# The routing of a two-block transformer kernel: router product, ranks, row copies and the first expert load rearranged

## The chip, the cores and the metric

The kernel runs on one NeuronCore of one Trainium2 chip. A core has five engines that run beside each other and meet at semaphores: TensorE (PE: matrix products and transposes, into PSUM), VectorE (DVE), ScalarE (ACT), GpSimd (POOL) and SyncE (SP, which here only issues DMAs). ACT and POOL issue DMAs too. On-chip data lie in SBUF (128 partitions); PSUM has eight banks of 128 x 512 floats. The metric is the time of one execution on the device in microseconds (us).

## The reference, cut to what matters

Two blocks of two layers each run over 512 tokens of width 1024. The first block is an attention and Fourier mixer and a long convolution, each with a dense feed-forward part. The second block's two layers end in a mixture of experts with two-level routing, which the kernel computes twice (i = 0, 1):

```python
pg = softmax(hf @ router_g)                       # (512, 4), top-1 group
gi = argmax(pg)
le = (hf @ router_e).reshape(t, 4, 8)             # 32 experts in 4 groups of 8
pk, ik = top_k(softmax(le[gi]), 2)                # two experts in the chosen group
wts = pg[gi] * pk / sum(pk);  eid = gi * 8 + ik
order = argsort(flat_e)                           # 1024 (token, expert) pairs, sorted by expert,
dest = start_pad[se] + arange(n) - start_raw[se]  # packed into blocks of 128 rows of one expert
yb = map(lambda xi, e: (silu(xi @ w1[e]) * (xi @ w3[e])) @ w2[e], blocks)
y = segment_sum(yb * buf_w, buf_tok)
```

## The kernel before, in words

Every engine has its own program, written as a list of stages. Between two stages that are not `joined`, the four computing engines meet: each drains, adds one to `stage_end` and waits until all have done so. SP runs ahead and loads weights into a ring of four slots of 2 MB.

At the end of each mixer stands `Project` (output matrix, 512 x 1024 results added to x), then `Norm` (an RMS norm with modulation, from x to h), then `Route`, `Experts` and `Combine`. Before the change `Project` and `Norm` are joined, and a meeting stands between `Norm` and `Route`.

Activations lie transposed, as eight tiles of 128 channels by 512 tokens. `Norm.scalar` ends with one ACT operation for each tile of h (L535), which adds one to `tiles`.

`Route`, on the engines:

- ACT issues two DMAs for the router weights (1024 x 4 and 1024 x 32; L2489, L2490), does the two exponentials (L2492, L2494), stores h by rows in DRAM as `h_rows` (L2496), and at the end reads the table of pairs back (L2499).
- PE makes the logits with a 128 x 128 piece of h stationary and the 36 router columns moving: 4 token tiles x 8 k = 32 products of 36 columns (L2529). Then it turns h into rows (32 transposes in 8 groups of 4, L2537). After the choice of experts it makes the rank of each token within its expert: 10 products for "how many tokens before me" and 4 for the totals (L2542, L2545).
- DVE copies the logits from PSUM (L2587), takes the group maximum, and then copies the 8 groups of rows from PSUM (L2594) before it goes on with the choice: a chain of small operations, each followed by a drain (helpers at L2561 to L2572). After `hot_done` it waits for the ranks (L2635), works out where each pair goes (`dest_done`), and then, once `h_rows` is stored, the plan: which expert each of up to 40 blocks has, and how many steps there are (L2663).
- POOL writes number tables and zeros, fills the table in DRAM (L2515), and after `dest_done` scatters the 8 x 128 pairs into it (8 indirect DMAs, L2520).

`Experts` then handles two blocks a step: POOL gathers 128 token rows (L2780), PE turns them (L2850), ACT and DVE split activations and weights into a rounded high part and a low rest (L2924, L2934 on ACT; L554, L3006 on DVE), and PE does three products for each (L560). SP's loads of w1, w3 and w2 (2 MB each, L2746) start once all engines have met; the second waits until the first gather has landed. In the first routing POOL sends two scatters with nothing to write ahead of its first gather, which set the counts of the semaphores right.

`L` numbers in the rows are those of the kernel before.

## Time and profile before

| | us |
|---|---|
| median of 3 runs | 4682.4 (4681.4 to 4684.97) |
| the profiled execution, its own time | 4681.74 |
| its span in the profile | 4679.9 |
| PE busy | 3998.8 (85%) |
| DVE busy | 2899.0 (62%) |
| ACT busy | 1916.4 (41%) |
| POOL busy | 880.0 (19%) |

The span is what the profiler saw from the first to the last instruction; 1.8 us lie around it. The granted clock of TensorE is printed as a share of 2.4 GHz, so 0.50 is 1.2 GHz. An idle time in square brackets stands before the instruction of the row, with what ended it. A queue name with q (ACTq, SPq) is the engine's sequencer issuing a DMA: the duration is that of the issue. A matrix product or transpose in full fp32 precision may appear as two MATMUL records.

### The profile page before, as it was taken

To read this page: it belongs to the slowest core of one execution; us is meant where nothing else is said; L and a number is where in the kernel's file an instruction comes from. 1 tells how busy PE (TensorE), PEld (TensorE's weight loads), DVE (VectorE), ACT (ScalarE), POOL (GpSimd) and SP (SyncE) were. 2 spreads that over 40 slices of the span, in tenths; PEclk is the share of its full clock that TensorE was granted. 3 is DMA by queue.
4 is the path that set the end of the run, shared out by engine and by line. 5 is a ranking of instruction groups with operands and counts; after the bars stand their busy time and mean duration, and the time that the engine had idled before them with its cause. 6 is when DMAs were issued, how large, how long until landed. Compare 5 with 4: busy or idle time off the path is not lost. (4 is left out here: it accounts for less than half of the span.)

```text
span 4679.9 us, 52688 instructions
## 1 busy us (share of the span) xinstructions
PE 3998.8 (85%) x19060; PEld 3186.2 (68%) x19060; DVE 2899.0 (62%) x3435; ACT 1916.4 (41%) x2295; POOL 880.0 (19%) x460
## 2 busy tenths in 40 slices
PE   4988899778988999678888888769999695899995
PEld 3755677536645777578888888548888474788884
DVE  6754775337745874344444445459999443899995
ACT  2142432203103332343333333247777221777773
POOL 0200000002100000032222221025554001355551
PEclk9989999969999999789999999879999796999997
DMA  5421354303501452100000001079998311999993
GB/s 184 144 91 36 113 177 143 110 13 127 215 18 63 164 170 86 31 19 18 18 18 18 18 18 36 8 271 376 355 365 331 126 54 33 373 376 360 366 357 111
DMA packets 372150, 691.39 MB, mean 148 GB/s; under 512 B 38327, under 2 KB 118327, under 8 KB 371320
## 3 DMA queue, kind: packets, MB, share of 16 engines
q1 hardware_dynamic: 327696, 639.79, 38.5%
q10 hardware_dynamic: 25032, 32.98, 2.1%
q0 software_dynamic: 19296, 16.94, 1.1%
q8 instruction: 80, 1.31, 0.1%
q14 instruction: 46, 0.38, 0.0%
HBM read 700.01 MB, written 41.00 MB: 158 GB/s over the span
## 5 line engine op out<-in xcount | busy, mean ns | idle before, releaser
L560 PE MATMUL psum<-work_rounded 128*128 128x512 f32 x3504 | 1164.1, 402 | 94.7 <-DVE work_rounded L554 29.0
L554 DVE TENSOR_TENSOR ring_rounded<-ring,work_rounded 128x2048 fp32r<-128x2048 f32 (+1 forms) x445 | 816.0, 1836 | 408.8 <-ACT work_rounded L549 279.7
L560 PEld LDWEIGHTS psum<-work_rounded 128*128 128x128 f32 x3504 | 669.2, 192 | 266.2 <-issue 114.9
L560 PE MATMUL psum<-work_rounded,fixed_rounded 128*128 128x512 f32 x2544 | 782.5, 402 | 28.0 <-DVE fixed_rounded L3006 15.8
L560 PE MATMUL psum<-work_rounded,ring_rounded 128*128 128x512 f32 (+1 forms) x1824 | 726.0, 398 | 0.0
L549 ACT ACTIVATE work_rounded<-ring 128x1024 fp32r<-128x1024 f32 x204 | 214.5, 1057 | 1026.3 <-PE psum L560 697.9
L2924 ACT ACTIVATE work_rounded<-ring 128x2048 fp32r<-128x2048 f32 x256 | 490.9, 1919 | 274.9 <-PE psum L560 171.2
L560 PEld LDWEIGHTS psum<-work_rounded,fixed_rounded 128*128 128x128 f32 x2544 | 483.1, 190 | 146.4 <-issue 15.9
L560 PE MATMUL psum<-fixed_rounded,work_rounded 128*128 128x512 f32 (+1 forms) x1088 | 432.1, 397 | 0.0
L560 PEld LDWEIGHTS psum<-work_rounded,ring_rounded 128*128 128x128 f32 x1824 | 350.8, 192 | 78.5
L554 DVE TENSOR_TENSOR work_rounded<-work,work_rounded 128x2048 fp32r<-128x2048 f32 (+1 forms) x196 | 337.6, 1733 | 41.9 <-ACT work_rounded L2924 37.5
L370 DVE SCALAR_TENSOR_TENSOR work<-ring,fixed,work 128x512 f32<-128x512 f32 x392 | 318.7, 825 | 25.9 <-issue 0.9
L560 PE MATMUL psum<-ring_rounded,fixed_rounded 128*128 128x512 f32 x768 | 307.2, 400 | 0.0
L2924 ACT ACTIVATE work_rounded<-work 128x2048 fp32r<-128x2048 f32 x128 | 245.2, 1919 | 101.2 <-PE psum L560 82.9
L2786 POOL DMA_INDIRECT pair_rows<-work x66 | 174.0, 2637 | 562.0 <-DVE work L3016 560.0
L554 POOL TENSOR_TENSOR ring_rounded<-ring,ring_rounded 128x1024 fp32r<-128x1024 f32 x32 | 89.7, 2807 | 906.1 <-ACT ring_rounded L549 906.1
L560 PE MATMUL psum<-ring_rounded 128*128 128x512 f32 (+1 forms) x768 | 239.7, 373 | 9.2 <-DVE fixed_rounded L554 9.2
L560 PEld LDWEIGHTS psum<-fixed_rounded,work_rounded 128*128 128x128 f32 x1088 | 209.4, 192 | 47.4 <-issue 2.6
L554 POOL TENSOR_TENSOR ring_rounded<-ring,fixed_rounded 128x1024 fp32r<-128x1024 f32 x23 | 48.2, 2099 | 976.1 <-ACT fixed_rounded L549 976.1
L2780 POOL DMA_INDIRECT fixed<-h_rows,work x64 | 170.7, 2667 | 54.7 <-POOL work L2777 53.8
L2163 PE MATMUL psum<-work 128*128 128x128 f32 x1152 | 156.9, 279 | 26.8 <-ACT work L2266 26.8
L560 PEld LDWEIGHTS psum<-ring_rounded,fixed_rounded 128*128 128x128 f32 x768 | 146.4, 191 | 32.6
(317 smaller groups left out, 6029.9 us busy)
## 6 DMA issues: line engine op xcount, KB each, us to landing
ring<-in_w SPq DMA_DIRECT2D x128, 2048.0 KB, 13.8
work<-in_w SPq DMA_DIRECT2D x64, 2048.0 KB, 13.5
ring<-in_mod_w SPq DMA_DIRECT2D x24, 2048.0 KB, 8.6
ring<-in_ada_w SPq DMA_DIRECT2D x24, 2048.0 KB, 8.0
ring<-in_ffn_w_in SPq DMA_DIRECT2D x44, 1024.0 KB, 7.6
ring<-in_ffn_w_out SPq DMA_DIRECT2D x10, 2048.0 KB, 7.9
ring<-in_w_in_a SPq DMA_DIRECT2D x32, 512.0 KB, 6.0
ring<-in_hy_w_in SPq DMA_DIRECT2D x6, 2048.0 KB, 8.2
```

What stands on the lines that cost most here:

```text
L370: ins = dve.scalar_tensor_tensor(out=acc, in0=w[:, k, :], scalar=c.par(cond, k), in1=acc, op0=ALU.mult, op1=ALU.add)
L549: return act.activation(c.rounded(out), v, ACT.Copy)
L554: return eng.tensor_tensor(c.rounded(v), v, c.rounded(v_high), ALU.subtract)
L560: ins = pe.matmul(out, c.rounded(w), c.rounded(x), start=(start and i == 0), stop=(stop and i == 2))
L2163: ins = pe.matmul(c.pair(4 * l + 2, KEYS)[:, cols], A[:, t, :], TT[:, t, :], start=False, stop=True, skip_group_check=True)
L2780: pool.indirect_dma_start(self.g[:, b, :], None, self.c.d["h_rows"], bass.IndirectOffsetOnAxis(ap=self.gi[:, b:b + 1].bitcast(U32), axis=0 ...
L2786: pool.indirect_dma_start(self.c.d["pair_rows"], bass.IndirectOffsetOnAxis(ap=self.si[:, b:b + 1].bitcast(U32), axis=0), self.y_sb[:, b, : ...
L2924: act.activation(c.rounded(self.unit_high(o, u)), self.unit_raw(o, u), ACT.Copy).then_inc(self.made, 1)
```

## The change: the routing's products, copies and first load

- **Router product.** The 36 router columns become the stationary side and the 512 tokens of a tile of h stream past them: 8 products of 512 columns, each of which waits only for its own tile of h. The result has 36 partitions; DVE copies it to SBUF (`lg_rows`), and PE turns it in 4 transposes back to 128 tokens by 36, which DVE copies again. The router weights are fetched by ACT at the start of `Project.scalar`, into the buffer of the gathered rows (`M_G`), and `Norm` is joined to `Route`.
- **Rows.** The 8 copies of h's rows from PSUM move from DVE to ACT, four before the second exponential and four behind it.
- **Ranks.** DVE sums the one-hot choices over token tiles (4 small additions, `sums`), and two products of 160 and 128 columns replace the 14.
- **First load.** A new semaphore `planned` follows the plan; SP waits for that alone before it asks for the first w1 matrix, and for the meeting only after it. The plan's scratch no longer lies in the rows' buffer, so DVE doesn't wait for the store.
- **POOL.** It waits for the 8 router products before it clears `M_G`. In the first `Experts` the two empty scatters go behind the first two gathers.

```diff
@@ Project.scalar
+        if self.route:
+            self.route.fetch(act)
         c.arrived(act, self.n[0])
         self.parts.open_high(act, self.unit(0), self.unit(1))
@@ Route
-        self.rw = v(R_W, KD, 36)
+        self.rw = v(M_G, KD, 36)
+        self.lg_rows = v(M_HI, T)
+    def keep_rows(self, act, i):
+        act.wait_ge(self.turned, self.base["turned"] + i + 1)
+        act.activation(self.ht[:, i // 2, 512 * (i % 2):512 * (i % 2) + 512], self.c.ps[:, i % 4, :], ACT.Copy)\
+            .then_inc(self.turned_out, 1)
@@ Route.scalar
-        act.dma_start(self.rw[:, :, 0:GROUPS], ...).then_inc(self.w, 16)
-        act.dma_start(self.rw[:, :, GROUPS:36], ...).then_inc(self.w, 16)
         act.wait_ge(self.gsub, self.base["gsub"] + 1)
         act.activation(self.eg, self.eg, ACT.Exp).then_inc(self.gexp, 1)
+        for i in range(4):
+            self.keep_rows(act, i)
         act.wait_ge(self.esub, self.base["esub"] + 1)
         act.activation(self.e8, self.e8, ACT.Exp).then_inc(self.eexp, 1)
+        for i in range(4, 8):
+            self.keep_rows(act, i)
@@ Route.gpsimd
+        pool.wait_ge(self.logits, self.base["logits"] + 1)
@@ Route.tensor
-        for t in range(NT):
-            for k in range(KD):
-                ins = pe.matmul(c.ps[:, 6, 36 * t:36 * t + 36], c.h[:, k, P * t:P * t + P], self.rw[:, k, :],
-                                start=(k == 0), stop=(k == KD - 1))
+        for k in range(KD):
+            pe.wait_ge(self.norm.tiles, self.norm.tiles0 + k + 1)
+            ins = pe.matmul(c.ps[0:36, 6, :], self.rw[:, k, :], c.h[:, k, :], start=(k == 0), stop=(k == KD - 1))
+        ins.then_inc(self.logits, 1)
+        pe.wait_ge(self.rowed, self.base["rowed"] + 1)
+        for t in range(NT):
+            ins = pe.transpose(c.ps[:, 7, 36 * t:36 * t + 36], self.lg_rows[0:36, P * t:P * t + P],
+                               c.const("ident")[0:36, 0:36])
         ins.then_inc(self.logits, 1)
...
-        for t in range(NT):
-            for b in range(t + 1):
-                pe.matmul(c.ps[:, 7, 32 * t:32 * t + 32], c.const("before" if b == t else "ones"), self.both[:, b, :],
-                          start=(b == 0), stop=(b == t))
-        for t in range(NT):
-            ins = pe.matmul(c.ps[:, 7, 128:160], c.const("ones"), self.both[:, t, :], start=(t == 0), stop=(t == NT - 1))
+        pe.matmul(c.ps[:, 5, 0:32 * (NT + 1)], c.const("ones"), self.sums.rearrange("p t e -> p (t e)"),
+                  start=True, stop=False, skip_group_check=True)
+        ins = pe.matmul(c.ps[:, 5, 0:32 * NT], c.const("before"), self.both.rearrange("p t e -> p (t e)"),
+                        start=False, stop=True, skip_group_check=True)
@@ Route.vector
-        dve.tensor_copy(self.lg, c.ps[:, 6, 0:36 * NT].rearrange("p (t n) -> p t n", t=NT))
+        dve.tensor_copy(self.lg_rows[0:36, :], c.ps[0:36, 6, :]).then_inc(self.rowed, 1)
+        dve.memset(self.sums[:, 0, :], 0.0)
+        dve.wait_ge(self.logits, self.base["logits"] + 2)
+        dve.tensor_copy(self.lg, c.ps[:, 7, 0:36 * NT].rearrange("p (t n) -> p t n", t=NT))
...
-        for i in range(8):
-            dve.wait_ge(self.turned, self.base["turned"] + i + 1)
-            dve.tensor_copy(self.ht[:, i // 2, 512 * (i % 2):512 * (i % 2) + 512], c.ps[:, i % 4, :]).then_inc(self.turned_out, 1)
...
+        for t in range(NT):
+            tt(self.sums[:, t + 1, :], self.sums[:, t, :], self.both[:, t, :], ALU.add)
         dve.drain().then_inc(self.hot_done, 1)
...
-        dve.wait_ge(self.stored, self.base["stored"] + 16)
...
+        dve.drain().then_inc(self.planned, 1)
@@ Experts.sync
-        sp.wait_ge(self.c.stage_end, 4 * self.number)
+        sp.wait_ge(self.route.planned, self.route.base["planned"] + 1)
         first, more = self.steps(sp)
         load(0, first, 0, 0, True)
+        sp.wait_ge(self.c.stage_end, 4 * self.number)
         load(0, first, 0, 1, True, self.gather[0])
@@ Experts.gpsimd
-        if self.i == 0:
-            for b in range(2):
-                self.scatter_rows(pool, b)
...
         for b in range(2):
             self.gather_block(pool, 0, first, b)
+        if self.i == 0:
+            for b in range(2):
+                self.scatter_rows(pool, b)
@@ stages
-        project.norm = add(Norm(..., after=project))
-        add(Route(c, i))
+        project.norm = add(Norm(..., after=project), joined=True)
+        route = project.route = Route(c, i, project.norm)
+        add(route)
```

The order of TensorE's instructions at the first routing, from the last product of the norm (L471 in both) to the first transposes of `Experts`, in the kernel before:

```order
L471 MATMUL psum<-work,fixed 128x512 x5
L2529 MATMUL psum<-work,fixed 128x36 x32
L2537 MATMUL psum<-fixed 128x128 x32
L2542 MATMUL psum<-work,fixed 128x32 x10
L2545 MATMUL psum<-work,fixed 128x32 x4
L2703 TENSOR_LOAD work
L2703 ISA x2
L2850 MATMUL psum<-fixed 128x128 x8
```

The same place in the changed kernel:

```order
L471 MATMUL psum<-work,fixed 128x512 x5
L2548 MATMUL psum<-fixed 36x512 x8
L2552 MATMUL psum<-fixed,work 128x36 x4
L2560 MATMUL psum<-fixed 128x128 x32
L2563 MATMUL psum<-work,fixed 128x160
L2565 MATMUL psum<-work,fixed 128x128
L2726 TENSOR_LOAD work
L2726 ISA x2
L2873 MATMUL psum<-fixed 128x128 x8
```

32 router products of 36 columns became 8 of 512 and 4 transposes, and 14 rank products became two. ACT at the same routing, in the kernel before, from the last tiles of the norm (L535) on:

```order
L527 ACTIVATE work<-psum,fixed 128x512
L535 ACTIVATE fixed<-fixed 128x512 x8
L2489 DMA work<-in_router_g_2 128x8x4
L2490 DMA work<-in_router_e_2 128x8x32
L2492 ACT_TABLE_LOAD
L2492 ACTIVATE work<-work 128x16
L2494 ACTIVATE work<-work 128x32
L2496 DMA h_rows<-work 128x4x1024
L2499 DMA work<-table 128x42x2
```

In the changed kernel, there:

```order
L527 ACTIVATE work<-psum,fixed 128x512
L535 ACTIVATE fixed<-fixed 128x512 x8
L2505 ACT_TABLE_LOAD
L2505 ACTIVATE work<-work 128x16
L2499 ACTIVATE work<-psum 128x512 x4
L2509 ACTIVATE work<-work 128x32
L2499 ACTIVATE work<-psum 128x512 x4
L2513 DMA h_rows<-work 128x4x1024
L2516 DMA work<-table 128x42x2
```

The two DMAs of the router weights are gone from here (they stand ahead of the first L549 of `Project`), and the eight copies of 512 columns came in around the second exponential.

## Rows read from the trace of the kernel before

**Rows 1.** Stretches: us, busy PE, PEld, DVE, ACT, POOL; clock; DMA share; GB/s
```profile
3124.00:3142.00 18.00, 18.00 (x86) 14.76 (x85) 16.59 (x12) 13.94 (x11) 4.95 (x3) 1.00 1.04 396
3011.30:3028.77 17.47, 13.95 (x66) 13.98 (x67) 0.00 (x1) 1.30 (x2) 4.72 (x8) 0.50 0.09 12
```
**Rows 2.** Timeline of ACT, first routing: start, duration, instruction [idle before, releaser]
```profile
3005.57 5.75 ACT L535 ACTIVATE fixed<-fixed 128x512 f32<-128x512 f32 x8 [4.23 <-DVE fixed L503]
3011.43 0.40 ACTq L2489 DMA_DIRECT2D work<-in_router_g  x1
3011.86 0.60 ACTq L2490 DMA_DIRECT2D work<-in_router_e  x1
```
**Rows 3.** Timeline of PE, first routing
```profile
3014.82 13.84 PE L2529 MATMUL psum<-work,fixed 128*128 128x36 f32 x64 [14.21 <-DMA work<-in_router_e]
...
3046.22 4.48 PE L2542 MATMUL psum<-work,fixed 128*128 128x32 f32 x20 [12.15 <-DVEq L2631]
3050.51 1.90 PE L2545 MATMUL psum<-work,fixed 128*128 128x32 f32 x8
```
**Rows 4.** Timeline of DVE, first routing
```profile
3028.77 0.31 DVE L2587 COPY work<-psum 128x144 f32<-128x144 f32 x1 [19.01 <-PE psum L2529]
3029.15 0.17 DVE L2572 TENSOR_REDUCE work<-work 128x4 f32<-128x16 f32 x1
3029.40 0.17 DVE L2591 TENSOR_TENSOR work<-work 128x16 f32<-128x16 f32 x1
3029.60 0.69 DVE L2594 COPY work<-psum 128x512 f32<-128x512 f32 x1
...
3035.20 0.40 DVE L2572 TENSOR_REDUCE work<-work 128x4 f32<-128x16 f32 x2
...
3052.44 0.19 DVE L2635 COPY work<-psum 128x32 f32<-128x32 f32 x1 [6.35 <-PE psum L2545]
...
3061.87 0.18 DVE L2663 CAST work<-work 128x41 int32<-128x41 f32 x1
```
**Rows 5.** Lines L464 and L471, 512 columns: ns min/median/max, first and last start
```profile
L464 PE MATMUL psum<-fixed x5: 1011/1061/1061, 62.0 to 65.4; 128*128 128x512 f32 x5
...
L471 PE MATMUL psum<-work,fixed x10: 592/592/692, 2996.1 to 3000.0; 128*128 128x512 f32 x10
```
**Rows 6.** Stretches after PE starts on the first expert block, each routing
```profile
3092.65:3097.40 4.75, 4.75 (x12) 3.75 (x13) 0.50 (x1) 1.78 (x1) 0.19 (x1) 0.51 1.04 385
3989.40:3995.10 5.70, 5.70 (x14) 4.50 (x15) 1.83 (x2) 3.30 (x2) 0.00 (x0) 0.51 1.05 392
```
**Rows 7.** Timeline of POOL, end of each routing and start of the experts
```profile
3058.45 1.62 POOL L2520 DMA_INDIRECT table<-work  x1 [41.64 <-DVEq L2651]
...
3075.47 0.10 POOL L2803 MEMSET work<- 128x2 int32 x1 [6.56 <-ACTq L3200]
3077.30 1.00 POOL L2786 DMA_INDIRECT pair_rows<-work  x1 [1.72 <-issue]
...
3080.69 1.07 POOL L2780 DMA_INDIRECT fixed<-h_rows,work  x1 [0.90 <-POOL work L2777]
...
3108.61 2.79 POOL L2780 DMA_INDIRECT fixed<-h_rows,work  x1 [0.85 <-POOL work L2777]
...
3972.60 1.07 POOL L2780 DMA_INDIRECT fixed<-h_rows,work  x1 [0.89 <-POOL work L2777]
```
**Rows 8.** Timelines of PE and ACT, the first expert block of each routing
```profile
3086.78 1.97 PE L2850 MATMUL psum<-fixed 128*128 128x128 f32 x8 [34.38 <-DMA fixed<-h_rows,work]
3085.51 3.71 ACT L2924 ACTIVATE work_rounded<-ring 128x2048 fp32r<-128x2048 f32 x2 [45.86 <-DMA ring<-in_w]
...
3095.62 1.91 ACT L2924 ACTIVATE work_rounded<-ring 128x2048 fp32r<-128x2048 f32 x1 [5.42 <-DMA ring<-in_w]
...
3979.93 1.97 PE L2850 MATMUL psum<-fixed 128*128 128x128 f32 x8 [32.50 <-DMA fixed<-h_rows,work]
...
3991.80 1.91 ACT L2924 ACTIVATE work_rounded<-ring 128x2048 fp32r<-128x2048 f32 x1 [4.89 <-DMA ring<-in_w]
```

More of the change, by code:

```diff
@@ L649, in __init__ @@
         self.gate, self.keep = gate, keep
-        self.norm, self.leads = None, True
+        self.norm, self.leads, self.route = None, True, None
         self.tiles, self.tiles0 = core.shared("x_tile", KD)
@@ L2427 @@
 R_W = R_HT + NT * D
[L2428 to L2429 removed]
+R_SM = R_W
+R_END = R_SM + 4000
 M_KEEP = W0 + WORK - 256
@@ L2447, with __init__ @@
 class Route(Stage):
-    def __init__(self, core, i):
+    def __init__(self, core, i, norm):
         super().__init__(core)
-        self.i = i
-        self.per = {"w": 32, "turned": 8, "turned_out": 8, "stored": 16, "logits": 1, "gsub": 1, "gexp": 1,
+        self.i, self.norm = i, norm
+        self.per = {"w": 32, "turned": 8, "turned_out": 8, "stored": 16, "logits": 2, "rowed": 1, "gsub": 1, "gexp": 1,
                     "esub": 1, "eexp": 1, "rank": 1, "filled": 16, "placed": 128, "back": 16,
-                    "hot_done": 1, "dest_done": 1, "vals_done": 1}
+                    "hot_done": 1, "dest_done": 1, "vals_done": 1, "planned": 1}
         self.base = {}
@@ L2479, in __init__ @@
         self.both = new(NT, EXPERTS)
+        self.sums = new(NT + 1, EXPERTS)
         self.destf = new(2, NT)
@@ L2651, in vector @@
         dve.drain().then_inc(self.dest_done, 1)
-        planf, cmp = new(48), c.view(R_HT, BLOCKS, EXPERTS)
-        dve.wait_ge(self.stored, self.base["stored"] + 16)
+        planf, cmp = new(48), c.view(M_HI + T, BLOCKS, EXPERTS)
         tt(cmp, row(ends, BLOCKS, EXPERTS), col(iota[:, 0:BLOCKS], EXPERTS), ALU.is_le)
@@ L2674, with __init__ @@
     ROOM = 12
-    def __init__(self, core, i, weights):
+    def __init__(self, core, i, weights, route):
         super().__init__(core)
-        self.i = i
+        self.i, self.route = i, route
         self.w1, self.w3, self.w2 = (core.d[w][i] for w in weights)
```

21 lines of the change are left out of this document (11 added, 10 removed).

## The prediction, made before the changed kernel was run

> **What bounds the kernel now.** I read the stretches first. In the steady expert loop TensorE is busy 18.00 of 18.00 us at full clock [rows 1], so it is the bound there, and whatever the loop's start gains is kept to the end. During the router product the same view shows PE busy 13.95 of 17.47 us at clock 0.50, DVE idle and DMA at 0.09 [rows 1]: no overlap, one engine at a time. So I went on to the timelines of the routing, where everything is a chain: ACT finishes the tiles of h (3005.57 + 5.75 = 3011.32), issues the router DMAs, PE multiplies, DVE chooses, PE ranks, DVE places, POOL scatters, all meet, and the experts start with a matrix that is not there yet. ACT idles 45.86 us until the first w1 lands at 3085.51 and PE 34.38 us until the first gather lands at 3086.78 [rows 8]. The whole of this is on the path, so a microsecond cut from it is a microsecond of the result, twice, since there are two routings.
>
> **Logits.** Before: PE starts at 3014.82, after the router weights have come, and DVE has the logits at 3028.77 [rows 3, 4]. After: the weights are there, and the first product can start when tile 0 is done. ACT's eight tiles take 5.75 us, 0.72 each and the last one a little longer [rows 2], so tile 0 is there at about 3006.4. A product of 512 columns in fp32 is two records. At the slow clock records start (65.4 - 62.0)/4 = 0.85 us apart, at the fast clock (3000.0 - 2996.1)/9 = 0.43 [rows 5]: 1.7 or 0.86 us a product. Which clock? PE has been idle since the norm's last product (started 3000.0, 0.6 long), and in the stretch before the logits the clock is 0.50, 1.2 GHz [rows 1]. When the first expert block starts after such a pause, the clock stays at 0.51 for 4.75 us in one routing and 5.70 in the other [rows 6], and then is at 2.4 GHz. In between them and a somewhat earlier rise (this stream has no gaps) I take 4.3 us. Then 5 records go at 0.85, the other 10 steps at 0.43, and the last lasts 0.6: 4.3 + 4.3 + 0.6 = 9.2 us, until 3015.6. Behind it come DVE's copy from PSUM (0.69, as L2594 [rows 4]), four small transposes, some 0.7, and four crossings of 0.11 (PE ends at 3028.66, DVE starts at 3028.77 [rows 3, 4]) less the overlaps: DVE copies the logits at 3017.2. Gain 28.77 - 17.2 = **11.6 us**. Ends: never a fast clock, 15 x 0.85 + 1.06 = 13.9 us, gain 6.5; always fast, 15 x 0.43 + 0.6 = 7.1, gain 13.8. The end "always fast" needs the clock not to fall in the 5.7 us pause.
>
> The Trainium skill (TensorE: Matmul & The Clock Gate, "What's actually happening") says that the slow state is the default and that activity releases it, at a moment that varies with where the stream begins. Rows 6 agree: 4.75 and 5.70 us for the same code.
>
> **Rows copied by ACT.** DVE's copies lie between 3029.57 (end of L2591) and 3035.20 [rows 4], 5.63 us. What was hidden under them now shows: the wait for the first exponential, two crossings and an operation of 0.17, together 0.4. Gain **5.2 us**. On ACT four copies must be over when DVE asks for the second exponential, about 17 small operations of 0.25 us (3029.15 to 3029.40 [rows 4]) or 4.2 us after the first. Four copies at ACT's pace of 0.72 [rows 2] take 2.9 and PE turns the rows beside them, so they fit. The other four run beside some 7 us of DVE's chain. If they didn't fit, the cost is one or two copies, 1.4 us. The store of h_rows goes out earlier than before in any case.
>
> **Ranks.** From 3046.22 to 3052.44, 6.2 us [rows 3, 4]. 28 records in 6.2 us are 0.22 each. The new ones are four: two of 160 columns and two of 128; by the slow clock of rows 5 (0.85 for 512) 0.27 and 0.21, in all 1.0, plus 0.2 to drain. Gain **5.0**. Against it stand four additions on DVE with their drains, 4 x 0.25 = **1.0**. The memset of 32 columns lies beside the transposes.
>
> So the point where POOL starts its scatters (3058.45 [rows 7]) comes 11.6 + 5.2 + 5.0 - 1.0 = 20.8 us earlier, in both routings: 41.6. POOL's own clearing now starts with the products' end instead of 3011.4, but has 18 us until POOL is needed.
>
> **The first w1.** The plan is done at 3062.05 [rows 4], and stays at that distance behind the placing. SP waited for the meeting at about 3075.4 [rows 7] and the matrix landed at 3085.51, 10.1 us later [rows 8]. With the same 10.1 it now lands at 3072.2 on the old scale, before the meeting. ACT can split it at once; the experts then hang on the first gather and on w3, which SP asks for only when that has landed. Two costs and two gains:
> - POOL's scatters into the table run beside the 2 MB load. Below: nothing. Above: the last one can't be held beyond the landing of the matrix plus its own time, 3072.2 + 2 against the 3070 or so of before, 3.5 us. The packets are tiny and few, so I take 0.5, twice 0.5 = **-1.0**.
> - In the first routing the gather is issued at 3080.69 behind two empty scatters that begin at 3077.30; two of them are 2.3 us [rows 7]. It then lands 6.1 us after issue (3086.78), beside the matrix. Alone it should be faster: at least 1.07 to issue plus a quarter of the matrix's 8.5 us (a quarter of the bytes), 3.2; at most 6.1. I take 4.5: landing at 3078.4 + 4.5 = 3082.9, gain **3.8**. w3 follows it as before (8.8 us, 3086.78 to 3095.62 [rows 8]).
> - In the second routing there are no scatters: issue 3972.60, landing 3979.93. With 4.5 it is 2.8 earlier. w3 took 11.9 us there (3979.93 to 3991.80), which I put down to w1 still being under way; with the 8.8 of the first routing 3.1 less. Gain **5.9**.
> - PE's part: block 0 needs w1's products before w3's; with the gather at 3082.9 they have time. I count no more gain than w3's arrival gives: **+9.7** for both. Below: 0 if the gather isn't faster and w3 slower; above: 3.2 instead of 4.5 twice, +12.3.
>
> The Trainium skill (DMA: Bandwidth & Descriptors, "Queues, rings and completion order") says that a DMA engine goes round between its queues packet by packet. By that rule a scatter waits for a packet of the load and not for the load: the first cost would be near nothing, and the sum 1 us better. No row of this trace shows a scatter beside a load.
>
> A row speaks against the start: POOL's gather takes 1.07 us while DVE is idle, but 2.79 at 3108.61 while DVE splits weights [rows 7]. Now ACT splits w1 right after the meeting, and DVE follows some 2 us later, when the first gather is already issued and only the second and the scatters remain. If DVE were earlier, 1.7 us a routing are lost. The Trainium skill (GPSIMD Engine Reference, "8. Key points") names it: POOL shares its SBUF interfaces with DVE where DVE has two SBUF inputs.
>
> **The fetch.** The two DMA issues now stand ahead of ACT's first operation of `Project`, which starts right after a meeting or a mixer, with DVE and PE waiting for it: 3011.43 to 3012.46 is 1.03 us [rows 2], twice: **-2.1**. Below zero cost isn't possible; above, small-packet traffic beside nothing else costs nobody.
>
> **The sum.** 41.6 - 1.0 + 9.7 - 2.1 = 48.2 us. From the profiled execution's 4681.7 (span 4679.9 and 1.8 around it) that is 4633.5; the median is 0.7 above this execution, so 4634.
>
> **Rivals.**
> - *The slow clock holds.* TensorE stays at 1.2 GHz through both products, each 5.1 us longer: 4634 + 10 = 4644. For it: with 36 columns the clock stayed at 0.50 for 17 us [rows 1]. Against: those were short products, and the 512-column streams of rows 6 brought the clock up within 5.7 us.
> - *The early matrix gives nothing.* The gather takes its 6.1 us as before, w3 its time, and the scatters are held the full 3.5 us: 4634 + 9.7 - 2.3 + 6 = 4647. For it: w3, not w1, is what ACT waits for second, and the code still holds it back until the gather lands. Against: the gather had the matrix beside it before.
> - *Slower: the loop gets out of step.* The loads, released by PE and ACT, run at DMA share 1.04 beside a TensorE that is full [rows 1]. If the new order at the start leaves the loads one slot later for good, each of the 64 expert blocks waits for a matrix. From 48.2/64 = 0.75 us a block on, the change is slower; at 1 us a block the time is 4634 + 64 = 4698. Against: after the start ACT never waits for a load in the loop, and the slots are freed in an unchanged order.
>
> **Chances.** The forecast 0.78 (own range 4626 to 4641), the slow clock 0.09, no gain from the matrix 0.10, slower 0.03. The range for 8 in 10: low 4625 (fast clock 2.2 twice, the shorter gather 2.6, and some us more if the ranks start at the fast clock), high 4649, which takes in both faster rivals. What can be told from no change is 0.2%, 9.4 us: both mild rivals are clearly faster, so faster 0.95, same 0.02, slower 0.03.
>
> **What would show it.** In the changed profile: the 8 router products start before the last tile of the norm is done and end some 9 us later, with a clock change among them; DVE's copy of the 128 x 144 logits about 11 us sooner behind the norm; no 128 x 512 copies on DVE in the routing; two rank products in about 1.2 us; the first w1 issued before the meeting, so that ACT's first split of weights waits for the meeting alone; the next wait of ACT, for w3, about 9 us behind the gather. It is wrong if PE's products take nearly 14 us, if the last scatters or the table's reading take longer than the 17 us from first scatter to meeting, if `Project` starts much later than 1 us after its meeting, or if an expert period is no longer 18.0 us.

## Result: 41 us of the 48 forecast, ratio 0.991

The changed kernel takes 4642.72 us (median; 4642.01 to 4643.43) against 4683.68 (4681.4 to 4688.73) of the kernel before on the same chip: ratio 0.9911, 95% interval 0.9894 to 0.9928. A second comparison gave 4643.6 against 4683.89, ratio 0.9916 (0.9899 to 0.9933). The forecast was 4634, range 4625 to 4649. The gain is 41.0 us (40.3 the second time) where 48.2 were forecast. The time lies inside the stated range, but outside the 4626 to 4641 that the prediction gave to its own mechanism.

The profile after has a span of 4641.6 us, 38.3 less than before. Its rows answer to the groups of before in turn. First the stretches (columns as in [rows 1]): the first 4.06 us and the last 4.30 of the router products, and one period of the steady loop.

```profile
3012.64:3016.70 4.06, 4.06 (x5) 0.89 (x6) 3.22 (x6) 4.06 (x7) 0.00 (x0) 0.50 0.02 4
...
3017.70:3022.00 4.30, 4.26 (x10) 0.90 (x8) 0.00 (x0) 1.03 (x1) 0.00 (x0) 1.00 0.00 0
3124.00:3142.00 18.00, 18.00 (x86) 14.76 (x85) 16.59 (x12) 13.95 (x12) 9.34 (x5) 1.00 1.04 395
```

The loop is what it was (ACT starts on a block 17.98 us after the one before in both traces). During the router products PE no longer stands alone: ACT's tiles (4.06 us) and DVE's norm (3.22) lie beside them, and between the two stretches the clock has gone from 1.2 to 2.4 GHz, where it stayed at 0.50 before [rows 1]. ACT's timeline, first routing, with the same columns as [rows 2]:

```profile
3011.68 5.75 ACT L535 ACTIVATE fixed<-fixed 128x512 f32<-128x512 f32 x8 [4.23 <-DVE fixed L503]
...
3024.18 2.04 ACT L2499 ACTIVATE work<-psum 128x512 f32<-128x512 f32 x4
3029.42 0.23 ACT L2509 ACTIVATE work<-work 128x32 f32<-128x32 f32 x1 [3.19 <-DVE work L2632]
...
3060.54 0.37 ACTq L2516 DMA_DIRECT2D work<-table  x1
3066.95 3.71 ACT L2947 ACTIVATE work_rounded<-ring 128x2048 fp32r<-128x2048 f32 x2 [35.36 <-PEq L2864]
...
3081.62 3.71 ACT L2947 ACTIVATE work_rounded<-ring 128x2048 fp32r<-128x2048 f32 x2 [7.16 <-DMA ring<-in_w]
```

3011.68 is the zero of all distances below; before it was 3005.57 [rows 2]. The first split of w1 now waits for the meeting and no longer for a DMA [rows 8]; the second, of w3, still waits 7.16 us for one. PE's timeline, answering to [rows 3] and [rows 8]:

```profile
3012.64 9.32 PE L2548 MATMUL psum<-fixed 128*36 128x512 f32 x16 [5.92 <-ACT fixed L535]
3022.74 0.44 PE L2552 MATMUL psum<-fixed,work 36*128 36x36 f32 x4 [0.78 <-DVE work L2608]
...
3037.28 0.90 PE L2563 MATMUL psum<-work,fixed 128*128 128x160 f32 x2 [10.35 <-DVEq L2654]
3037.98 0.64 PE L2565 MATMUL psum<-work,fixed 128*128 128x128 f32 x2
...
3071.86 1.54 PE L2873 MATMUL psum<-fixed 128*128 128x128 f32 x6 [33.25 <-DMA fixed<-h_rows,work]
```

Sixteen records in 9.32 us, and both rank products over in 1.3. (The last row is cut where its window ends: the block's eight transposes take 1.97 us, as before.) DVE's, answering to [rows 4]:

```profile
3023.22 0.31 DVE L2611 COPY work<-psum 128x144 f32<-128x144 f32 x1 [0.49 <-PE psum L2552]
...
3025.05 1.09 DVE L2589 TENSOR_SCALAR work<-work 128x16 f32<-128x16 f32 x1
...
3038.65 0.19 DVE L2658 COPY work<-psum 128x32 f32<-128x32 f32 x1 [1.50 <-PE psum L2565]
```

The logits are copied 11.54 us behind the zero (before 23.20), the ranks 26.97 (before 46.87). POOL's, answering to [rows 7]:

```profile
3024.30 1.81 POOL L2531 MEMSET work<- 128x2048 f32 x1
...
3044.66 1.62 POOL L2539 DMA_INDIRECT table<-work  x1 [17.12 <-DVEq L2674]
...
3054.17 0.96 POOL L2539 DMA_INDIRECT table<-work  x1 [0.30 <-issue]
3065.48 0.10 POOL L2827 MEMSET work<- 128x2 int32 x1 [10.35 <-ACTq L3224]
...
3067.70 1.08 POOL L2804 DMA_INDIRECT fixed<-h_rows,work  x1 [0.94 <-POOL work L2801]
```

A table of the distances, in us from the start of the norm's tiles on ACT, each read from a timeline's start. "Step 2's first block" is ACT's start on the activations of the third expert block (L2934 before, L2957 after); from there on the steady loop runs.

| | before | after | moved |
|---|---|---|---|
| logits copied, 1st / 2nd routing | 23.20 / 23.05 | 11.54 / 10.76 | 11.66 / 12.29 |
| first scatter issued | 52.88 / 52.21 | 32.98 / 31.24 | 19.90 / 20.97 |
| table read back | 64.99 / 63.94 | 48.86 / 46.80 | 16.13 / 17.14 |
| first gather issued | 75.12 / 71.11 | 56.02 / 53.97 | 19.10 / 17.14 |
| PE turns the first block | 81.21 / 78.44 | 60.18 / 57.33 | 21.03 / 21.11 |
| ACT splits the first w3 | 90.05 / 90.31 | 69.94 / 67.42 | 20.11 / 22.89 |
| step 2's first block | 120.39 / 121.76 | 101.43 / 99.81 | 18.96 / 21.95 |

From first scatter to the table's reading the kernel gives 3.8 us back in each routing (12.11 and 11.73 before, 15.88 and 15.56 after). A second profile of the changed kernel has 15.36 and 15.43 there, so 3.3 to 3.8; its step 2 begins at 101.43 and 99.84, within 0.03 us of the first profile's. That is the largest difference from the forecast, and the experiments began there.

### The profile page after: what moved, and what is told of

Read it like the earlier page. It is cut to its first block and busy times, and to the rows that moved or that the text cites. A ratio compares the mean times of both kernels' runs of the same rounds, so it can differ in the third digit from the quotient of the medians.

```text
span 4641.6 us, 52428 instructions
## 1 busy us (share of the span) xinstructions
PE 3979.8 (86%) x18924; PEld 3153.0 (68%) x18924; DVE 2889.9 (62%) x3431; ACT 1924.3 (41%) x2311; POOL 885.9 (19%) x460
## 3 DMA queue, kind: packets, MB, share of 16 engines
q10 hardware_dynamic: 25032, 32.98, 2.1%
## 5 line engine op out<-in xcount | busy, mean ns | idle before, releaser
L549 ACT ACTIVATE work_rounded<-ring 128x1024 fp32r<-128x1024 f32 x204 | 214.6, 1057 | 1029.3 <-PE psum L560 698.0
L2947 ACT ACTIVATE work_rounded<-ring 128x2048 fp32r<-128x2048 f32 x256 | 490.9, 1919 | 260.4 <-PE psum L560 175.3
L2947 ACT ACTIVATE work_rounded<-work 128x2048 fp32r<-128x2048 f32 x128 | 245.2, 1919 | 101.3 <-PE psum L560 83.0
```

The lines of the kernel that those rows point to most:

```text
L549: return act.activation(c.rounded(out), v, ACT.Copy)
L2947: act.activation(c.rounded(self.unit_high(o, u)), self.unit_raw(o, u), ACT.Copy).then_inc(self.made, 1)
```

## Experiments

"Gain" is against the kernel before on the same chip. The intervals of the ratios are some 8 us to either side, so small differences between kernels are read from the distances in their traces. `e1` to `e4` were compared with one set of runs of the kernel before, median 4687.68, and gain some 2 to 4 us more than the changed kernel's 41.0 and the distances of their step 2 give; their gains are not compared with those of the changed kernel.

| run | median us | gain | ratio, 95% |
|---|---|---|---|
| `e1_w1_late` | 4647.31 | 40.4 | 0.9915 (0.9898 to 0.9932) |
| `e2_w1_after_scatters` | 4639.37 | 48.3 | 0.9899 (0.9883 to 0.9916) |
| `e3_w3_free` | 4638.66 | 49.0 | 0.9896 (0.9880 to 0.9913) |
| `e4_warm_clock` | 4641.90 | 45.8 | 0.9907 (0.9890 to 0.9923) |
| `e5_w1_scat_w3_free` | 4632.75 | 51.1 | 0.9891 (0.9874 to 0.9907) |
| `e6_warm_blocks` | 4633.78 | 50.1 | 0.9893 (0.9876 to 0.9909) |
| `e7_dve_rows` (one run) | 4649.9 | 34.0 | |
| `e8_clear_moved` (one run) | 4641.51 | 43.2 | |
| `e9_best` | 4629.23 | 55.5 | 0.9878 (0.9862 to 0.9895) |
| `e10_old_products` (one run) | 4661.17 | 23.6 | |
| `e11_best_no_norm_warm` | 4630.05 | 54.7 | 0.9883 (0.9867 to 0.9900) |

### The first w1 behind the meeting again

```diff
     def sync(self, sp):
-        sp.wait_ge(self.route.planned, self.route.base["planned"] + 1)
+        sp.wait_ge(self.c.stage_end, 4 * self.number)
         first, more = self.steps(sp)
         ...
         load(0, first, 0, 0, True)
-        sp.wait_ge(self.c.stage_end, 4 * self.number)
```

> The changed kernel with the first w1 asked for after the meeting again. Theory A (the early 2 MB load holds back the completion of the table's scatters): from the first scatter to the reading of the table 12.1 us as in the kernel before, not 15.9 as in the changed one, so the meeting comes 3.8 us sooner; against it the first gather again runs beside w1 (6 to 7 us from issue to TensorE's first transpose, not 3.4 to 4.2), and w3 follows it. Net in the first routing about 2.7 us sooner at the first block, in the second about 1.9 us later, so the total is within 2 us of the changed kernel's 4642.7. Rival B (the later reading of the table has another cause, such as the order on GpSimd or the earlier store of the rows): the 15.9 us stay, and all of the start's gain is lost, some 8 us slower than the changed kernel, 4650.

From first scatter to the table's reading it takes 12.04 and 11.75 us, as before the change: the 3.8 us are the load's. At the start of the experts it loses what the scatters win: step 2's first block begins at 102.60 and 100.99, 1.2 us later than in the changed kernel in both routings, and from the gather's issue to PE's turn is 8.15 and 7.03 us in place of 4.16 and 3.36. PE turns the first block within 0.3 us of when it does in the changed kernel; it is ACT that then waits for w1, whose split starts 1.5 and 2.9 us behind that turn. A first routing 2.7 us sooner, as expected, is not there. So the early matrix, as the change has it, is worth 1.2 us a routing and not the 4 to 5 forecast.

### The first w1 behind the last scatter

```diff
         sp.wait_ge(self.route.planned, self.route.base["planned"] + 1)
+        sp.wait_ge(self.route.placed, self.route.base["placed"] + 16 * 8)
```

> The changed kernel with the first w1 asked for when the plan is there and the eight scatters have landed. Theory A: 12.1 us from the first scatter to the reading of the table; w1 asked for at about the same moment, landing some 4 us behind the meeting, while the gather has it beside it only for its last 2 us. First block about 3 us sooner in each routing than in the changed kernel: 4636 to 4638. Rival B (another cause of the late reading): 15.9 stay and w1 comes later for nothing, 4644 or more. Rival C: the load now holds back the reading of the table instead (from 4.9 us to 7 or more), and the total stays at 4642.

The view of DMA issues, for the changed kernel in the stretch with the first routing's scatters (count, KB each, median us from issue to landing):

```profile
table<-work POOLq DMA_INDIRECT x8
work<-table ACTq DMA_DIRECT2D x1, 42.0 KB, 4.9
```

and for this one:

```profile
table<-work POOLq DMA_INDIRECT x8, 2.6
work<-table ACTq DMA_DIRECT2D x1, 42.0 KB, 6.0
```

The median landing of 2.6 us is that of scatters with no load beside them; for the changed kernel the view gives no figure. In this kernel the eight take 12.05 and 11.74 us again. The load now meets the next small transfer instead: the table's reading takes 6.0 us in place of 4.9 in the first routing (POOL is at the gather 8.27 us after it, before 7.16); in the second, where the load starts a little later behind it, nothing is lost (7.34 against 7.17). Step 2's first block begins 0.47 and 3.61 us sooner than in the changed kernel, where 3 were expected in each routing. PE's turn is 2.29 and 2.84 us sooner; in the first routing 1.82 of that is lost behind it, with 19.4 us at 1.2 GHz up to step 2 in place of 13.7.

The changed kernel's DMA while the load lies on the scatters (columns of [rows 1]; the last two are DMA share and GB/s):

```profile
3049.80:3052.00 2.20, 0.00 (x0) 0.00 (x0) 0.00 (x0) 0.00 (x0) 1.59 (x3) 0.50 0.81 15
...
3054.00:3058.00 4.00, 0.00 (x0) 0.00 (x0) 0.00 (x0) 0.00 (x0) 0.96 (x1) 0.50 1.05 374
3058.00:3060.50 2.50, 0.00 (x0) 0.00 (x0) 0.00 (x0) 0.00 (x0) 0.00 (x0) 0.50 0.39 117
```

POOL's issues keep their pace (0.96 us each, the last at 3054.17), so POOL isn't held; the packets are. The trace's records of single DMA packets show it. Each scatter has 32. Those of the first four come 1.5 to 2.2 us behind their issue, the last of them at 3050.86. The load's packets begin at 3050.88. The fifth scatter is issued at 3050.38, but none of its packets comes before 3056.16, 4.2 us late; the 128 packets of the last four scatters then lie among the load's. The last of them is at 3059.86, the last of the load at 3059.85. In the second routing the same gap goes from 3924.50 to 3930.08, and the ends are 3933.22 and 3933.64; there the load, issued at 3923.82, has its first packet only at 3926.93, later than the fifth scatter was due by its issue. With the load behind the scatters all eight come 1.27 us apart without a gap. So the scatters end with the load. This is the bound that the prediction worked out (3.5 us: "beyond the landing of the matrix") and set aside.

### The first w3 without its wait for the gather

```diff
-        load(0, first, 0, 1, True, self.gather[0])
+        load(0, first, 0, 1, True)
```

> The changed kernel with w3 asked for right after the meeting, not after the first gather. Theory A: w3 is what the first block waits for: ScalarE starts to split it 10 to 11 us after the meeting and not 16; the gather beside it takes 6 us and not 4. Products of w1 begin 2 us later, those of w3 follow without a pause: 2 to 3 us sooner in each routing, 4637 to 4639. Rival B (the gather, not w3, decides): the slower gather costs 2 us in each routing, 4646 or more.

ACT's timeline of the first routing, L2947 being the splits of w1 and of w3:

```profile
3066.20 3.71 ACT L2947 ACTIVATE work_rounded<-ring 128x2048 fp32r<-128x2048 f32 x2 [34.96 <-PEq L2864]
...
3077.22 3.70 ACT L2947 ACTIVATE work_rounded<-ring 128x2048 fp32r<-128x2048 f32 x2
```

w3's split waits for no DMA any more, and the gather pays: 7.81 and 7.08 us from issue to PE's turn in place of 4.16 and 3.36. In all, step 2's first block begins 2.25 and 2.29 us sooner. From PE's turn to that block are 35.78 and 36.29 us, against 41.25 and 42.48 in the changed kernel. The clock differs too: in the first routing of the changed kernel it falls twice more after the first slow stretch, in this kernel once; in all it is at 1.2 GHz for 10.5 and 11.2 us in place of 13.7 and 18.4.

The changed kernel from PE's first turn on:

```profile
3071.80:3079.00 7.20, 6.53 (x19) 5.22 (x20) 2.98 (x3) 1.20 (x2) 4.45 (x5) 0.52 0.83 267
3079.00:3085.30 6.30, 3.21 (x14) 2.25 (x12) 1.73 (x1) 3.68 (x2) 0.00 (x0) 1.00 1.04 381
3085.30:3088.80 3.50, 2.80 (x7) 2.25 (x8) 2.76 (x2) 1.91 (x3) 0.00 (x0) 0.53 1.05 386
3088.80:3099.30 10.50, 6.96 (x35) 5.44 (x34) 6.88 (x6) 7.94 (x6) 3.52 (x3) 0.99 1.04 399
3099.30:3102.30 3.00, 3.00 (x8) 2.30 (x7) 3.00 (x2) 0.94 (x2) 0.00 (x0) 0.50 1.05 388
```

PE is busy 3.21 of 6.30 us while it waits for w3, and behind that the clock is at 1.2 GHz again for 3.5 us; after a stretch with 6.96 of 10.50 it is there again for 3. Here the gap cost its own length, and slow products stand behind it.

What the slow stretches cost can be read from the kernels that have the same expert code and load order as the changed one. From PE's first turn to step 2 they take, by routing:

| kernel | us | of these at 1.2 GHz |
|---|---|---|
| `e8_clear_moved` | 40.11 / 42.60 | 11.3 / 18.7 |
| changed | 41.25 / 42.48 | 13.7 / 18.4 |
| changed, second profile | 41.52 / 42.63 | 14.1 / 18.5 |
| `e7_dve_rows` | 41.36 / 41.51 | 13.9 / 14.0 |
| `e4_warm_clock` | 43.24 / 43.70 | 19.2 / 19.9 |
| `e10_old_products` | 43.68 / 43.31 | 19.9 / 19.3 |

The changed kernel's two rows of these stretches:

```profile
3071.86:3113.11 41.25, 33.30 (x129) 26.32 (x130) 25.95 (x17) 23.73 (x18) 7.91 (x8) 0.83 1.01 371
3944.38:3986.86 42.48, 34.84 (x129) 27.42 (x130) 26.36 (x17) 23.73 (x18) 6.86 (x6) 0.78 1.00 371
```

The same work takes 3.6 us longer where 8.6 us more of it ran at 1.2 GHz. A line through the twelve gives 0.36 us for each slow microsecond, and none of them lies more than 0.4 us from it. Between the first routing of `e8_clear_moved` and the second of `e4_warm_clock` PE's busy time grows from 32.4 to 35.2 us, so most of the 3.6 us is slower products and not longer waits. This is an estimate from a comparison of traces; no kernel changed the clock there and nothing else.

### Both loads changed

The two edits above together.

> The changed kernel with w1 asked for when the eight scatters have landed, and w3 right after the meeting. Theory A (the load holds back the scatters, and w3's late request lets TensorE's clock fall inside the first block): the two gains add up, 3.8 us from the scatters and 3 to 6 us from w3, less 2 us since w1 now lands after the meeting: 5 to 8 us a routing, some 12 us under the changed kernel. Rival B (both take their gain from the same wait): no more than either alone, 5 to 7 us under the changed kernel in all.

Step 2's first block begins at 97.74 and 94.16, 3.69 and 5.65 us sooner than in the changed kernel: 9.3 us, where the two edits by themselves give 4.1 and 4.5. So they about add up. The median is 10.85 us below that of the changed kernel on the same chip. The rest of the forecast is here: 51.1 us against 48.2.

### Five idle products ahead of the router's

```diff
         pe.wait_ge(self.w, self.base["w"] + 32)
+        for _ in range(5):
+            pe.matmul(c.ps[:, 7, :], c.const("ones"), c.x[:, 0, :], start=True, stop=True)
         for k in range(KD):
```

> The changed kernel with five unneeded 512-column products (4.3 us at the fast clock) on TensorE ahead of the router products, in the norm's pause; nothing reads what they write. Theory A (the clock term of the sum is right): the clock stays at 1.00, the 8 router products end some 1 us behind the last tile, and the logits are there 2.1 us sooner than in the changed kernel (9.4 us behind the start of the norm's tiles, not 11.5), 4 us in all: 4638 to 4639. Rival B (the tiles, not the clock, set the end of the products): under 0.7 us a routing, 4642.

The stretch of its router products:

```profile
3007.35:3017.54 10.19, 8.92 (x25) 2.45 (x24) 5.78 (x11) 7.03 (x9) 1.07 (x6) 1.00 0.00 0
```

and PE's timeline there:

```profile
3009.22 7.07 PE L2550 MATMUL psum<-fixed 128*36 128x512 f32 x16 [0.49 <-ACT fixed L535]
```

The clock is 1.00 throughout, the 16 records take 7.07 us in place of 9.32, and the logits are copied at 9.19 in both routings, 2.35 and 1.57 sooner. PE's first turn is still 2.15 and 1.56 us sooner. But step 2's first block begins only 0.16 and 0.34 us sooner, and no total of 4 us less, as expected, can be read from that. The start of the experts gives it back: from PE's first turn to that block are 43.24 and 43.70 us (changed kernel 41.25 and 42.48), of which 19.2 and 19.9 at 1.2 GHz (13.7 and 18.4).

### Idle products at the start of the experts

The first w3 freed as above, and these products, of the same kind as ahead of the router's:

```diff
+        idle_products(5)
         turn(first, 0)
+        idle_products(2)
         hidden(first, 0)
```

> The changed kernel with w3 asked for right after the meeting (as in the run with w3 free) and seven unneeded 512-column products on TensorE, five ahead of the first expert block's transposes and two behind them; nothing reads them. Theory A (the clock at the start of the first blocks costs about half of its 10 to 11 slow us): from the first transpose to the third block's split 32 to 34 us, against 36 with w3 free alone, so 2 to 4 us less a routing, if the five products don't delay the transposes. Rival B (the start is bound by loads and splits, not by TensorE's clock): 36 us as before, or more by what the extra products take.

Its stretches from PE's first turn:

```profile
3070.97:3088.97 18.00, 15.53 (x72) 11.86 (x72) 10.54 (x7) 12.39 (x11) 3.44 (x5) 0.99 1.05 390
3088.97:3095.47 6.50, 5.43 (x13) 4.28 (x14) 6.50 (x6) 3.07 (x3) 1.44 (x2) 0.50 1.05 391
```

The slow stretch at the start is gone. One of 6.8 us comes later, in both routings; in the kernel without idle products the later one lasts 3.4. Step 2's first block begins 1.26 and 1.68 us sooner than there, 0.36 and 0.54 of it before PE's first turn. From that turn it is 34.88 and 35.15 us, against 35.78 and 36.29: 0.9 and 1.1 us less, where 2 to 4 were expected if the clock costs half of its slow time. Compared with it by the medians (gains 50.1 and 49.0) nothing can be told.

### The row copies back on DVE

```diff
-        for i in range(4):
-            self.keep_rows(act, i)
 ...
+        for i in range(8):
+            dve.wait_ge(self.turned, self.base["turned"] + i + 1)
+            dve.tensor_copy(self.ht[...], c.ps[:, i % 4, :]).then_inc(self.turned_out, 1)
```

> The changed kernel with the eight copies of the rows back on VectorE. Theory A (the copies cost VectorE what they took before): from the copy of the logits to the second exponential 10.4 us, not 6.2 in the first routing and 5.0 in the second, so 4.5 to 5.5 us a routing longer, and some 10 us in all, 4653. Rival B (with TensorE's faster clock at that moment the copies are shorter or partly hidden): under 3.5 us a routing.

DVE's timeline has them again:

```profile
3023.66 4.87 DVE L2614 COPY work<-psum 128x512 f32<-128x512 f32 x8
```

From the first exponential to the second are 8.89 and 8.55 us in place of 5.36 and 4.14, step 2's first block begins 3.33 and 3.37 us later, and the time is 6.3 us above the changed kernel's on the same chip. The forecast had 5.2 a routing for the move; isolated, it is worth 3.5 and 4.4, where 4.5 to 5.5 were expected. The eight copies take 4.87 us here and took 5.69 in the kernel before, where three of them waited for PE's transposes.

### POOL's clearing moved

DVE's TENSOR_SCALAR at 3025.05 takes 1.09 us, and the same one in the second routing 0.17. POOL clears 2048 columns of `work` beside it in the first routing alone. The edit delays the other clearing (of `fixed`, L2529 after) until the ranks are made, so that the one of `work` comes earlier:

```diff
-        pool.memset(c.view(M_G, 2, D), 0.0)
         if self.i == 0:
 ...
         pool.wait_ge(self.filled, self.base["filled"] + 16)
+        pool.wait_ge(self.hot_done, self.base["hot_done"] + 1)
+        pool.memset(c.view(M_G, 2, D), 0.0)
```

> The changed kernel with one of POOL's two clearings (the 2 x 1024 columns that the experts' plan uses) moved from beside DVE's first operations to behind the ranks. If the DVE operation of 128 x 16 that took 1.09 us was held by POOL's clearing, it takes 0.17 again in the first routing, and from the first exponential to the second is 4.4 us in place of 5.36; total 4643.6 - 0.9 = 4642.7. Rival: it was held by the other, which stays (the zeros for the output), or by ACT's copies: 1.09 stays.

DVE and then POOL in the first routing:

```profile
3023.24 0.17 DVE L2590 TENSOR_SCALAR work<-work 128x16 f32<-128x16 f32 x1
```

```profile
3020.75 1.80 POOL L2530 MEMSET work<- 128x2048 f32 x1
...
3034.64 1.80 POOL L2536 MEMSET fixed<- 128x2048 f32 x1 [10.66 <-DVEq L2655]
```

The operation takes 0.17 us again, from first to second exponential it is 4.44 in place of 5.36, as expected. It was the clearing of `work` that lay on it, though: in the changed kernel it runs from 3024.30 to 3026.11 and the DVE operation ends at 3026.14; here it is over at 3022.55, before DVE comes to that place. ACT's copies lie beside the operation in both, so they are not the cause. The expectation had the number right and named the wrong one of the two. Step 2's first block begins 2.17 us sooner in the first routing (99.26); 1.03 of that is there at PE's first turn, and behind it one slow stretch of the clock is missing. In the second routing, where nothing was to be won, it is 0.10 sooner.

### The old router products with the early weights

```diff
-        for k in range(KD):
-            pe.wait_ge(self.norm.tiles, self.norm.tiles0 + k + 1)
-            ins = pe.matmul(c.ps[0:36, 6, :], self.rw[:, k, :], c.h[:, k, :], ...)
+        pe.wait_ge(self.norm.tiles, self.norm.tiles0 + KD)
+        for t in range(NT):
+            for k in range(KD):
+                ins = pe.matmul(c.ps[:, 6, 36 * t:36 * t + 36], c.h[:, k, P * t:P * t + P], self.rw[:, k, :], ...)
```

> The changed kernel with the old router products: tokens stationary, 32 products of 36 columns behind the norm's last tile, all 144 logits copied at once; the router's weights still come early, and all else is as changed. PE then starts at about 5.9 us behind the start of the norm's tiles and takes 13.84 as before: logits at 19.8, against 11.54 (changed) and 23.2 (before). So 8.3 of the 11.66 us would be the form of the products and 3.3 the early weights: two routings, 4643.6 + 16.6 = 4660. Rival: the form brings nothing and all is the early weights (or the clock): logits at 11.5 to 13, total 4643 to 4647.

```profile
3014.84 13.84 PE L2549 MATMUL psum<-fixed 128*128 128x36 f32 x64 [10.85 <-ACT fixed L535]
```

This row of PE's timeline has the same 13.84 us as before [rows 3], behind the last tile and no longer behind a DMA. The logits are copied at 19.76 and 19.78, the total is 4661.17: in the first routing 3.4 of the 11.7 us are the early weights, 8.2 the form of the products with its overlap and its faster clock, which no run takes apart. PE's clock stays at 0.50 through them.

### All that helped, with and without the router's idle products

> All that helped, together: the first w1 asked for after the scatters, the first w3 without its wait for the gather, 5 idle 512-column products ahead of the router's and 5 + 2 at the start of the experts, and POOL's clearing of the plan's rows moved to behind the ranks. Sum of the single gains against the changed kernel (4643.6 in the last comparison): 10.85 for the first two, 2 x 1.5 for the products in the first blocks (block 2 began 1.26 and 1.68 us sooner than without them), 2.35 + 1.57 for the clock of the router products, 0.9 for the clearing: 18.7, so 4625. Rival: the clock gives back what the router's idle products gain, as when they stood alone (block 2 only 0.16 and 0.34 us sooner): 4625 + 3.4 = 4628 to 4629.

> The same without the 5 idle products ahead of the router's. If the gains of the clock add up it is 3.9 us slower than the version with them (4629); if the first blocks give that back, the two are within 1 us of each other, both at 4628 to 4629.

The version with both loads changed, the clearing moved and idle products at both places takes 4629.23 us, 55.5 less than the kernel before (ratio 0.9878) and 14.5 to 15.2 less than the changed kernel, by its two gains of 41.0 and 40.3. The single gains added up to 4625; with the idle products' share given back it was to be 4628 to 4629. Without the idle products ahead of the router it is 4630.05. So their 2.35 and 1.56 us are given back here too: step 2's first block begins at 94.50 and 90.56 with them, 94.34 and 90.78 without. In the first routing this isn't the clock. The table's reading is issued 2.50 us sooner with them, the gather behind it only 0.57, and PE's first turn is 0.16 later. The DMA issues of the version with them:

```profile
work<-table ACTq DMA_DIRECT2D x1, 42.0 KB, 8.2
```

The table's reading takes 8.2 us beside the load of w1, which goes out 1.5 us behind it. In the three other kernels with this distance it takes 6.0, 6.1 and 6.3; in the second routings, where the load goes out 2.0 us behind, 4.9 to 5.0. In the second routing PE's first turn is 1.62 us sooner, and that is lost behind it. The stretches of the version without them, from PE's first turn, have one slow spell left where the changed kernel has three, in the first routing; in the second there is none:

```profile
3070.67:3091.17 20.50, 16.95 (x78) 13.05 (x79) 14.17 (x11) 15.00 (x13) 4.77 (x5) 0.99 1.05 389
3091.17:3094.17 3.00, 3.00 (x9) 2.35 (x8) 3.00 (x2) 0.58 (x2) 0.00 (x0) 0.50 1.04 392
```

## Why the prediction was right, and where it wasn't

The path held, and so did the range; the gain was 7 us smaller than forecast, and one term was wrong in its mechanism. The time lies just outside the forecast's own 4626 to 4641 and nearest to the 4644 of the slow clock, a rival that did not happen. By its own steps, with both routings together:

- **Logits**, forecast 2 x 11.6, measured 11.66 + 12.29. The clock was forecast slow for 4.3 us and then fast; it was slow for 4.6 us of the products in the first routing, and for 3.1 in the second, whose products were over in 8.55. Both stretches of [rows 6] from which 4.3 was taken begin behind transposes, and not at PE's first work after the pause; that the mean came out so near is partly luck. The old products with the early weights show 3.4 us of this to be the weights and 8.2 the products.
- **Rows copied by ACT**, forecast 2 x 5.2, measured 4.45 + 4.92 against the kernel before, whose transposes ran at 1.2 GHz for their first 3.9 us. In the first routing 0.9 went to the operation of 1.09 us beside POOL's clearing. The prediction had called the clearing harmless because it had 18 us of room; it looked at POOL's own deadline and not at what ran beside it.
- **Ranks less sums**, forecast 2 x 4.0, measured 3.79 + 3.81. The point at which the scatters start moved by 40.9 of the 41.6 us forecast.
- **Scatters beside the load: the mis-sized term.** Forecast 2 x 0.5, measured 3.8 + 3.8 (3.3 + 3.7 in the second profile). It is the load alone: behind the meeting or behind the scatters, the 12.1 and 11.7 us are back. The prediction had bounded the term at 3.5 and then took the low end, on "The packets are tiny and few". Their packets did not slip in between the load's: for 5.3 and 5.6 us none came at all. By this the prediction's own sign of being wrong is there: from first scatter to the meeting are 20.8 us, where it allowed 17. The next small transfer, the table's reading, is slower beside the load too: 4.9 us alone, 6.0 to 8.2 with the load 1.5 us behind it.
- **Start of the experts**, forecast 9.7 (3.8 + 5.9). From the table's reading to step 2's first block the distances shrank by 2.83 and 4.81, 7.6 in all. The gather's share was fully there (6.09 to 4.16 and 7.33 to 3.36, forecast to 4.5 each). What was missing: w3 followed the gather in 9.76 and 10.09 us, where the forecast had 8.8 for both (8.84 and 11.87 before), and from w3's split to step 2 it took another 1.1 and 0.9 us more than before, with slow stretches behind the gap in which PE waited for w3. The kernel with w3 freed is the one that shortens this. The kernel with w1 late adds that w1's early load bought 1.2 us a routing net of the scatters.
- **Fetch**, forecast -2.1. The two issues stand in the changed trace at 2948.44 and 2948.87, 0.40 and 0.60 long, ahead of ACT's first operation of `Project`. That operation starts 1.05 us later than before in both routings (5.44 us behind ACT's last one in place of 4.39, and 17.47 us of idle in place of 16.41). By the start of the norm's tiles 0.8 and 0.4 of it are left. So the term was 1.2 and not 2.1.
- **Sum.** The scatters start 40.9 us sooner, their delay takes 7.6, the start of the experts gives 7.6: 40.9 us at step 2. Less 1.2 for the fetch that is 39.7. The profiled spans differ by 38.3, and by 40.5 with the second profile of the changed kernel; the medians differ by 41.0 and 40.3. The two profiles of the changed kernel stand 4.0 us apart already at `Project` of the first routing, ahead of everything that was changed, so how closely the sum meets one span is luck.

Of the rivals, "the slow clock holds" was wrong as put: the products did reach 2.4 GHz. "The early matrix gives nothing" came nearest in its mechanism: the scatters were held for the full bound and 0.3 us more, as it said, but the gather did get faster. Together they give 1.2 us a routing. "The loop gets out of step" did not happen: the period is 17.98 us in the changed trace too.

The Trainium skill (DMA: Bandwidth & Descriptors, "Queues, rings and completion order") was drawn on for a cost of near nothing, as DMA engines go round between queues packet by packet. The measured 3.8 us don't agree with that use of it. The packet records show where the time goes: the fifth scatter's packets start 4.2 us late, and only then do scatters and load alternate. What holds them for these 4.2 us stays open. The other page, on the interfaces that POOL shares with DVE (GPSIMD Engine Reference, "8. Key points"), was drawn on for DVE operations with two SBUF inputs; it names those in a 2-port mode beside them. Here one with a single input, beside POOL's clearing, took 1.09 us in place of 0.17, and ended 0.03 us behind the clearing. A reduction and an operation with two inputs just ahead of it, beside the same clearing, took their usual time. Which mode the slow one ran in, no run shows.

What also stays open is why the clock falls where it does in the first blocks. The runs show only that it falls behind stretches with gaps, and that a start that comes sooner can have more slow time (19.2 us in `e4_warm_clock`) or less (11.3 in `e8_clear_moved`).

## What to carry to other kernels

A large load that was started early took its price here from the small transfers that were on the path at that moment. Where the trace shows the same, ask for it behind the last of them, and if a bound says "not before the load has landed", cost it at that bound until a row shows less. A gain ahead of a phase that starts with gaps is worth only what is left at the phase's end; measure there, not at the edit. Here the start of the experts took 40.1 to 43.7 us for the same code, a spread of 3.6 us, more than the small gains ahead of it (2.35, 1.57, 0.9 us) and less than the 8.2 of the products. When an operation is moved beside others, look at what its neighbours on the other engines will now run against, and not only at whether it is in time.

## What the runs showed of the hardware that was not expected

- Eight indirect scatters of 128 rows, 12.1 and 11.7 us alone from the first issue to what waits for them, take 15.4 to 15.9 in the two profiles of the changed kernel, beside a 2 MB load, with POOL's issues unchanged at 0.96 us each. None of their packets came for 5.3 and 5.6 us from about the load's issue on, and the last came with the load's last, within 0.01 us in the first routing and 0.4 before it in the second.
- A read of 42 KB in small pieces took 4.9 us alone, 6.0 to 8.2 in four kernels with a load issued 1.5 us behind it, and 4.9 to 5.0 in the same kernels with the load 2.0 us behind.
- Streams of 512 columns behind an idle of 5.92 us brought the clock from 1.2 to 2.4 GHz 4.6 and 3.1 us after they began, for the same code; streams of 36 columns left it at 1.2 GHz for all their 13.84.
- In the first blocks the clock fell behind a stretch in which PE was busy 3.21 of 6.30 us, and stayed down for 3 to 7 us a time. Over twelve starts of the experts with the same code, 11.3 to 19.9 us at 1.2 GHz went with 40.1 to 43.7 us in all.
- Products whose results nobody reads kept the clock up at their own place, but the gain (2.35 and 1.57 us ahead of the scatters) did not reach the steady loop in two kernels out of two, in one of the four routings because of the table's reading and not of the clock.
